# Conditioning vector of a two-block decoder kernel: sums over partitions as two wide products of rounded parts with ones, two projection groups later

## The reference, cut to what matters

```python
mod = jax.nn.silu(c) @ ada_w[l] + ada_b[l]                      # (1, 6 * 1024)
sh1, sc1, g1, sh2, sc2, g2 = [m[:, None, :] for m in jnp.split(mod, 6, axis=-1)]
h = rms_norm(x, norm1_g[l]) * (1.0 + sc1) + sh1
x = x + g1 * (mixed @ w_out[l])
h2 = rms_norm(x, norm2_g[l]) * (1.0 + sc2) + sh2
x = x + g2 * y.reshape(B, S, D)
```

## Time and profile before

| | us |
|---|---|
| median of 3 runs | 2003.45 |
| lowest and highest | 2002.98, 2004.38 |
| the profiled execution's own time | 2001.61 |
| its span in the trace | 1999.8 |
| TensorE busy in the span | 1959.1 |
| VectorE, ScalarE, GpSimd busy | 1366.6, 792.1, 847.1 |
| mean granted clock of TensorE | 0.998 of full |

### The profile page before, as it was taken

One profiled execution on the slowest core, in us unless ns is written; L12 is line 12 of the kernel. 1 busy time (PEld: TensorE's weight loads), 2 busy tenths in 40 slices (PEclk: granted clock), 3 DMA queues, 4 the chain that ended last, 5 costly groups with the idle time before them and its releaser, 6 DMA issues.

```text
span 1999.8 us, 27882 instructions
## 1 busy us (share of the span) xinstructions
PE 1959.1 (98%) x9978; PEld 1442.9 (72%) x9978; DVE 1366.6 (68%) x3014; ACT 792.1 (40%) x1815; POOL 847.1 (42%) x678
## 2 busy tenths in 40 slices
PE   9999999999999999999999999999999999999998
PEld 7888876888868875788886766666666666666564
DVE  6742034333374567749999988888888888887777
ACT  3222223133563326621271566555556455510100
POOL 3544432427443753424524444443444435343332
PEclk9999999999999999999999999999999999999999
DMA  7655642515202411134479999999999999999999
GB/s 283 213 183 182 160 117 102 190 56 179 90 6 59 127 35 54 43 121 133 131 315 372 418 416 421 421 421 422 422 421 419 418 421 417 411 421 418 421 422 317
DMA packets 93788, 529.80 MB, mean 265 GB/s; under 512 B 10176, under 2 KB 14704, under 8 KB 44144
## 3 DMA queue, kind: packets, MB, share of 16 engines
q1 hardware_dynamic: 50544, 249.78, 33.7%
q0 software_dynamic: 37440, 270.02, 33.0%
q10 hardware_dynamic: 5696, 8.66, 2.1%
HBM read 521.08 MB, written 7.34 MB: 264 GB/s over the span
## 4 chain that ended last, share of the span: by engine, by line
PE 28%; DMA 26%; DVE 10%; POOL 4%; issue 2%; ACT 1%; DVEq 0%; ACTq 0%; POOLq 0%
DMA work<-in_peer_uv,consts 14%; DMA ring<-in_peer_uv,consts 12%; PE ps L905 9%; PE ps L1249 6%; PE ps L1318 4%; PE ps L1343 3%; DVE tables L2239 2%; DVE work L2214 2%; POOL ring L2958 2%; POOL work L2958 2%; DVE ring L2214 1%; PE ps L1210 1%; PE ps L955 1%; PE ps L1309 1%; PE ps L1258 1%
## 5 line engine op out<-in xcount | busy, mean ns | idle before, releaser
L1343 PE MATMUL ps<-work,tmp 128*128 128x512 f32 x1008 | 446.9, 597 | 15.7 <-DVE tmp L2279 15.5
L1318 PE MATMUL ps<-hT,work 128*128 128x256 f32 x1984 | 449.4, 381 | 0.0
L1318 PEld LDWEIGHTS ps<-hT,work 128*128 128x128 f32 x1984 | 374.3, 190 | 74.4 <-issue 29.6
L2856 POOL TENSOR_TENSOR w_lo<-ring,w_hi 128x1024 fp32r<-128x1024 f32 (+2 forms) x112 | 267.0, 2390 | 335.8 <-ACT w_hi L2361 317.3
L1343 PEld LDWEIGHTS ps<-work,tmp 128*128 128x128 f32 x1008 | 190.5, 191 | 238.3 <-issue 211.6
L2958 POOL DMA_INDIRECT work<-in_peer_uv,consts x130 | 203.3, 1564 | 283.6 <-DVE tables L2239 225.2
L2958 POOL DMA_INDIRECT ring<-in_peer_uv,consts x126 | 198.0, 1572 | 290.9 <-DVE tables L2239 258.4
L2361 ACT ACTIVATE w_hi<-ring 128x1024 fp32r<-128x1024 f32 (+2 forms) x116 | 120.5, 1042 | 362.9 <-PE ps L905 320.9
L2718 ACT ACTIVATE ring<-iota,consts 128x128 f16<-128x128 f32 x768 | 231.6, 427 | 0.0
L2771 ACT ACTIVATE hT<-hT 128x4 f32<-128x4 f32 (+1 forms) x66 | 13.6, 206 | 487.5 <-DVE hT L2214 487.5
L2214 DVE CUSTOM_DVE_ANT_0 work<-work,tables 128x1024 f32<-128x1024 f32 x130 | 158.0, 1221 | 66.1 <-DMA work<-in_peer_uv,consts 65.3
(11 more groups left out here) (395 smaller groups left out, 3154.2 us busy)
## 6 DMA issues: line engine op xcount, KB each, us to landing
work<-in_peer_v SPq DMA_DIRECT2D x64, 1024.0 KB, 9.1
work<-in_u_steps SPq DMA_DIRECT2D x62, 1024.0 KB, 9.0
ring<-in_a_w_in SPq DMA_DIRECT2D x48, 512.0 KB, 4.2
ring<-in_ada_w SPq DMA_DIRECT2D x48, 512.0 KB, 5.0
ring<-in_peer_w_q SPq DMA_DIRECT2D x32, 512.0 KB, 3.5
ring<-in_a_w_out SPq DMA_DIRECT2D x16, 512.0 KB, 4.1
ring<-in_b_w_in SPq DMA_DIRECT2D x16, 512.0 KB, 4.4
ring<-in_c_in SPq DMA_DIRECT2D x12, 512.0 KB, 3.7
```

What stands on the lines that cost most here:

```text
L1318: mm = pe.matmul(ps[:, 4 + s, j * DT:(j + 1) * DT], u[s][:, j, k, :], hT[:, k, GATHERED * P:T], start=(k == 0), stop=(k == KD - 1))
L1343: mm = pe.matmul(ps[:, 2 * t + half, :], tmp[:, s, j * DT + t * P:j * DT + (t + 1) * P], v_ring[:, s, j, half * BANK:(half + 1) * BANK], s ...
L2856: pool.tensor_tensor(w_lo[q % NPIECE][:, 0:n], ring[:, at:at + n], w_hi[q % NPIECE][:, 0:n], ALU.subtract).then_inc(w_split, 1)
```

## The change

1. **Two products in place of one or four.** VectorE's `ada_split(n)` rounds the sum y to fp32r (`ada_high(n)`) and subtracts (`ada_lo`), for all twelve groups. TensorE multiplies `ones_r` [128, 128] with both parts, 512 columns each, into one bank. `ones_r` is made once by VectorE at the start.
2. **Columns are picked out of the wide result.** `ada_out` for columns multiplies the [128, 512] result with the identity (repeated four times), reduces over 128 columns, and adds the bias: three dependent instructions in place of one.
3. **Two groups later.** `ADA_LAG` is 4: the pieces of `ada_w` lie between those of the fifth to twelfth projection group, and TensorE sums behind these. The pieces from group 8 on keep their place in the list.
4. **Room.** The parts lie in `ysum`, `spare` and `tables`, where `causal` was loaded at the start; `causal` is now loaded by SP with the first piece of `b_out`. The four loads of `x` share one semaphore.

```diff
-ADA_LAG = 2
+ADA_LAG = 4
...
+        ada_lo = [parts("ada_lo0", "ysum", 0, BANK), parts("ada_lo1", "spare", 0, BANK)]
+        ada_hi = [parts("ada_hi0", "tables", 3072, BANK), parts("ada_hi1", "tables", 2560, BANK)]
+        ones_r = parts("ones_r", "tables", 3584, P)
+        def ada_high(n):
+            return ada_hi[n == ADA_IN_A + 2]
...
+                if name == ("b_out", 0, 0):
+                    full(sp, "ada", 11)
+                    sp.dma_start(causal, ins["causal"]).then_inc(causal_loaded, 16)
...
             def ada(n):
-                part = ADA_ORDER[n] // 2
                 o = start("ada", n)
-                pe.wait_ge(ada_step, KD * (n + 1))
-                y = ada_sum[n % 2]
-                if part in (2, 5):
-                    mm = pe.matmul(o, ones[:], y[:], start=True, stop=True)
-                else:
-                    for i in range(4):
-                        mm = pe.matmul(o[:, i:i + 1], y[:, i * P:(i + 1) * P], ones[:, 0:1],
-                                       start=True, stop=True)
-                end(mm, "ada", n)
+                pe.wait_ge(ones_made, 1)
+                pe.wait_ge(ada_split_done, n + 1)
+                pe.matmul(o, ones_r, ada_high(n), start=True, stop=False)
+                end(pe.matmul(o, ones_r, ada_lo[n % 2], start=False, stop=True), "ada", n)
...
+            def ada_split(n):
+                y, hi = ada_sum[n % 2], ada_high(n)
+                dve.wait_ge(ada_step, KD * (n + 1))
+                if n >= 1 and ada_high(n - 1) is hi:
+                    full(dve, "ada", n - 1)
+                elif n >= 2 and ada_high(n - 2) is hi:
+                    full(dve, "ada", n - 2)
+                dve.tensor_scalar(hi, y[:], 1.0, None, ALU.mult).then_inc(ada_high_done, 1)
+                dve.wait_ge(ada_high_done, n + 1)
+                dve.tensor_tensor(ada_lo[n % 2], y[:], hi, ALU.subtract).then_inc(ada_split_done, 1)
...
-                    taken(dve.tensor_tensor(modcol[:, part, half * 4:half * 4 + 4], o[:, 0:4],
-                                            col("ada_b", part * KD + half * 4, 4), ALU.add), "ada", n)
+                    column = modcol[:, part, half * 4:half * 4 + 4]
+                    own = tmp[:, 0, :].rearrange("p (i c) -> p i c", c=P)
...
+                    taken(dve.tensor_tensor(own, o.rearrange("p (i c) -> p i c", c=P),
+                                            ident[:].unsqueeze(1).to_broadcast([P, 4, P]), ALU.mult), "ada", n)
+                    drained(dve, "ada", n)
+                    dve.tensor_reduce(column, own, AX.X, ALU.add).then_inc(ada_col, 1)
+                    dve.wait_ge(ada_col, 2 * n + 1)
+                    dve.tensor_tensor(column, column, col("ada_b", part * KD + half * 4, 4), ALU.add).then_inc(ada_col, 1)
...
             for n in range(12):
-                if 1 <= n < RET_H:
-                    ada(n - 1)
...
-                if RET_H <= n <= ADA_IN_A:
-                    ada(n - 1)
+                if n >= ADA_LAG - 1 and n <= ADA_IN_A + ADA_LAG - 2:
+                    ada(n - ADA_LAG + 1)
+                    ada_split(n - ADA_LAG + 1)
                 if ADA_LAG <= n < ADA_IN_A + ADA_LAG:
                     ada_out(n - ADA_LAG)
             ada(ADA_IN_A)
+            ada_split(ADA_IN_A)
```

More of the change, by code:

```diff
@@ L592, in network @@
         x_again = sem("x_again")
-        x_loaded = [sem(f"x_loaded{t}") for t in range(NT)]
+        x_loaded = sem("x_loaded")
         xT_loaded = [sem(f"xT_loaded{q}") for q in range(KD // 2)]
@@ L610, in network @@
         ada_step = sem("ada_step")
+        ones_made = sem("ones_made")
+        ada_high_done = sem("ada_high_done")
+        ada_split_done = sem("ada_split_done")
+        ada_col = sem("ada_col")
+        causal_loaded = sem("causal_loaded")
         mod_done = sem("mod_done")
@@ L829, in _ @@
             sp.wait_ge(stored, 16 * (DENSE + 2 * (GATHERED - 1)))
-            sp.wait_ge(row_loaded, 16 * 7)
+            sp.wait_ge(row_loaded, 16 * 6)
             sp.wait_ge(gate_bias, 16)
@@ L1436, in gate_columns @@
                 ada(ADA_IN_A + 3)
+                ada_split(ADA_IN_A + 3)
             def add_residual(name, n, xn, gate=None, between=None, ahead_of_last=None):
@@ L1485, in ada_out @@
                 else:
-                    taken(dve.tensor_tensor(modcol[:, part, half * 4:half * 4 + 4], o[:, 0:4],
-                                            col("ada_b", part * KD + half * 4, 4), ALU.add), "ada", n)
+                    column = modcol[:, part, half * 4:half * 4 + 4]
+                    own = tmp[:, 0, :].rearrange("p (i c) -> p i c", c=P)
+                    dve.wait_ge(const_loaded, 16)
+                    dve.wait_ge(qk_done, 4 * min(n + ADA_LAG + 1, RET_H))
+                    taken(dve.tensor_tensor(own, o.rearrange("p (i c) -> p i c", c=P),
[4 more added lines that the diff above has]
+                    dve.tensor_tensor(column, column, col("ada_b", part * KD + half * 4, 4), ALU.add).then_inc(ada_col, 1)
+            dve.wait_ge(made, 1)
+            dve.tensor_scalar(ones_r, ones[:], 1.0, None, ALU.mult).then_inc(ones_made, 1)
             dve.wait_ge(cols_loaded, 16)
@@ L1561, in _ @@
                 taken(dve.tensor_tensor(o_lo["a_out"][:, f, :], o, o_hi["a_out"][:, f, :], ALU.subtract), "zT_a", f)
-            ada(ADA_IN_A + 1)
-            ada(ADA_IN_A + 2)
+            for n in (1, 2):
+                ada(ADA_IN_A + n)
+                ada_split(ADA_IN_A + n)
             def last_gates():
@@ L1651, in _ @@
             for i, (part, g) in enumerate(((1, "n1_g"), (4, "n2_g"))):
-                for c in range(2):
-                    drained(dve, "ada", (2 if i == 0 else 6) + c)
+                dve.wait_ge(ada_col, 2 * (4 if i == 0 else 8))
                 dve.scalar_tensor_tensor(modcol[:, part, :], modcol[:, part, :], 1.0, col(g, 0, KD),
@@ L1842, in _ @@
             n_units = len(att_units)
+            dve.wait_ge(causal_loaded, 16)
             def att_scores(n):
@@ L2385, in _ @@
             act.dma_start(iota[:], ins["iota"]).then_inc(row_loaded, 16)
-            act.dma_start(causal, ins["causal"]).then_inc(row_loaded, 16)
             act.dma_start(trig[:], ins["trig"]).then_inc(row_loaded, 16)
```

8 lines of the change are left out of this document (4 added, 4 removed).

## The result

| | before | after |
|---|---|---|
| median of 4 runs each, on the same chip, us | 2003.28 | 2019.06 |
| lowest and highest | 2002.98, 2004.38 | 2016.54, 2020.38 |
| ratio, 95% interval | | 1.0078, 1.0065 to 1.0090 |
| the profiled execution's own time | 2001.61 | 2020.38 |
| its span | 1999.8 | 2018.6 |

The change makes the kernel 15.8 us **slower**; forecast were 6.8, and a time of 2010.2 in a range of 2002 to 2014. The direction, both waits and the size of the one in group 11 were right; the wait in the retention and the clock cost more than forecast, and the products gained less.

What follows compares the result with a forecast made beforehand. TensorE, busy 98%, was taken as the bound. -5.3 (products) + 4.3 (retention wait) + 6.1 (group 11 wait) + 1.7 (clock) = +6.8 us on 2001.61 gave 2008.4, as a median 2010.2; range 2002 to 2014.

Steps and rivals of the forecast that it cites:

- both waits: Likeliest case: TensorE waits in group 11 and at the retention's start; 2007.5 to 2014 us, chance 0.56.
- clock: Lower granted clock on TensorE behind the two longer waits: +1.7 us for both together, bounds 0 and 3.4.
- products: Cheaper column and gate sums on TensorE: -5.3 us, of which eight column sums 4.0; bounds -4.8 and -5.7.
- retention wait: TensorE waits for the first decayed scores while VectorE finishes group 8's sum: +4.3 us, bounds 3.5 and 6.3.
- group 11 wait: TensorE waits for ScalarE's first group 10 result, behind a load slowed by the bias table's DMA: +6.1 us, bounds 0 and 9.
- The rival that took the Trainium skill's rule on queues: Only the retention wait: queues share engines, piece (11, 2) lands in time; 2002.5 to 2004.2 us, chance 0.22.
- GpSimd has nearly no pieces left to split by then, so I stay at 4.3: Retention: GpSimd would not hold up VectorE's group 8 sum, so up to 2.0 us more was left out.
- landed 5.0 us later: Retention: group 8's fourth piece lands 5.0 us after its issue and is used at X + 10.8.
- issued at X + 4.3: Retention: group 8's fourth piece is issued 4.3 us after X, the time group 7's column result is ready.
- I take 1.7 for both together: Clock: the two longer waits together lose 1.7 us at the lower clock, though each can bring that.
- the first two gate sums save this in full: Gate sums on TensorE: 0.42 us saved on each of the first two, 0.8 us in all.
- No cost: Projection groups: 2.8 us more VectorE work in 21.8 costs nothing, as VectorE waits for pieces there.

Runs made afterwards that it cites:

- the run with both orders mended: Changed kernel with the bias table's DMA at group 1 instead of 9 and VectorE's group 8 sum ahead of group 7's columns: 2000.39 us, ratio 0.9987.
- the first run: Changed kernel with ADA_LAG back at 2 instead of 4, the new products kept: 2011.36 us, ratio 1.0046.
- the run with the old products: Kernel before with ADA_LAG = 4, the bias table's DMA at group 1 and group 8's sum ahead of group 7's columns: 2002.95 us, ratio 0.9997.

## Why the prediction was wrong in size

Terms of its sum, with what they measured:

| term | forecast | measured | from |
|---|---|---|---|
| products | -5.3 | -3.8 | old products against new, no waits: scores, `a_out`'s end |
| retention wait | +4.3 (3.5 to 6.3) | +8.2 | trace after |
| group 11 wait | +6.1 (0 to 9) | +5.8 | trace after |
| clock | +1.7 (0 to 3.4) | +4.2 | granted clock, trace after: 2.0 and 2.2 |
| not in the sum | 0 | +1.2 | trace after, against the run with both orders mended |

They give 15.6, which is how late `a_out`'s end is; 15.9 are in the traces at 1008 us and 15.8 in the medians. Of the last row 0.6 us is there at 140 us already, ahead of both waits (half of it the wait for ScalarE above), 0.3 comes at the ends of the two waits and 0.3 in `a_out`.

- **Group 11: right**, in mechanism and size. The piece was issued behind the same split, landed in 11.1 us (12 taken), and ScalarE's order made the stall. The rival that took the Trainium skill's rule on queues ("DMA: Bandwidth & Descriptors", section "Queues, rings and completion order": each DMA engine goes round-robin over its queues by packets) would have put 9 us for a load beside the table; here loads took 11 to 20 us, and from 230 to 240 us the other queue moved nothing.
- **Retention: the mechanism right, the term mis-sized by 3.9 us.** Three steps failed. "GpSimd has nearly no pieces left to split by then, so I stay at 4.3": one piece was left, of `a_out`, and it was split while VectorE worked on that sum's last piece, because its DMA is issued right beside that of the piece VectorE waits for. Holding it back took 2.1 us off the wait and left the forecast 4.3; in the changed kernel itself the hold-up is 2.96 - 1.54 = 1.4 us. The rule that the prediction cited and set aside (the Trainium skill, "SBUF — State Buffer", section "Who interferes with whom") is what happened: the sum by it would have been 2.0 higher. Then "landed 5.0 us later": here it took 6.9. In the runs with the table early or the results taken out first it was under 5 us; why it was slower here was not tried, and it may be this one execution. Last, "issued at X + 4.3": it was X + 5.1, since VectorE was through with the second piece only at 286.80 (X + 4.6) and SP's issue ahead of it (285.56) took 1.63 us instead of 0.43.
- **The clock: mis-sized by 2.5 us.** The step that failed is "I take 1.7 for both together": each wait had its own price, 2.0 and 2.2 us. The other runs have the same size behind every wait of 3 us and more, however long: 2.8 us behind one of 3.2 (the sum ahead of the evictions), 2.8 behind 4.3 (the subtraction held back), 2.9 behind 6.4 (the table early), 2.1 behind 6.3 (the sum of group 8 moved), 2.2 behind 17.3 (the table beside the third group); over all of them 1.7 to 3.0. The 1.7 of the earlier trace rows was not a sure price either. The wait of 1.9 us at that place stands in all thirteen traces (before, after and the eleven runs), and in eight of them the clock does not fall behind it: the 64 matmuls of the product take 14.05 us there, and 15.74 in the other five, before and after among them. (In the first run, too, the clock stays up behind a wait of 2.1 us, and a wait of 4.3 behind it costs 2.9.) TensorE in the run with both orders mended:

```profile
429.80 14.05 PE L1044 MATMUL ps<-ring,work 128*128 128x256 f32 x64 [1.95 <-DVE x_lo_b L1616]
```

  With one trace of each kernel it is open if this hangs on the kernel or on the execution.
- **Products: 1.4 too much.** The eight column sums gave 3.7 of 4.0. The four gate sums gave 0.1 to 0.2 instead of 1.3: behind the second gate TensorE waits 0.57 us in the fastest run for VectorE to take out a gate (L1507), and what the last two save goes into waits for the last token tile: the transposes start 4.5 us ahead of the run with the old products, but TensorE then waits 0.32 us for VectorE's normalised tile (L1439), and the product behind is 3.9 ahead. The step "the first two gate sums save this in full" failed.
- **"No cost" for VectorE's added work**: right for the change as made, from group 4 on. At the old place it costs. The later place looked like all loss in the prediction; the runs show that it is what gives the products room.
- **The range**: 2003.45 - 5.3 + 6.3 + 6.1 + 3.4 is 2013.95, and its upper end stopped there: it took the retention's and the clock's upper bounds as the limit, and both were exceeded (8.2 and 4.2), while the products came out below their lower one (4.8). It left out group 11's own upper bound of 9; with that and the products at 4.8 it would be 2017.4, still under the measured median.

## What to carry to other kernels

When a DMA is issued behind the use of another piece, price the wait as a chain: first piece used, next loaded, used; then look for what the neighbouring DMA of the same issue sets off on another engine at the same time. Work moved to another place keeps its gain only if every engine's fixed order is moved with it: here one call moved up by a line on VectorE and one DMA issued earlier were worth 18 us, eight times the 2.3 that are won in the end. And a wait of TensorE of 3 us or more cost a further 1.7 to 3.0 us here, since the clock behind it is half for some us; that price did not grow with the wait, so each further wait has to be given its own.

## What the runs showed of the hardware

- One large DMA on queue 10 (3 MB in rows of 1536 bytes) stretched the 512 KB loads of queue 1 to 11 to 20 us at both places where they stood beside it (from 230 to 240 us queue 1 moved no packet at all), and SP's own issue instructions took 3.2 to 4.5 us instead of 0.33 (228.09, 233.74 and 236.97 above).
- The lower clock behind a wait of TensorE cost 1.7 to 3.0 us for waits of 3.2 to 17.3 us, with no rise by length; behind one of 1.9 us it cost 1.7 us in five traces and nothing in eight.
- A GpSimd subtraction delays small instructions of VectorE as well. In the fastest run VectorE's addition of 128x4 (usually 0.16 us) took 2.17 while GpSimd subtracted (VectorE's row, then GpSimd's):

```profile
275.30 2.17 DVE L1518 TENSOR_TENSOR modcol<-modcol,cols 128x4 f32<-128x4 f32 x1
```

```profile
275.11 2.34 POOL L2890 TENSOR_TENSOR w_lo<-ring,w_hi 128x1024 fp32r<-128x1024 f32 x1 [3.62 <-ACT w_hi L2396]
```
